# One queue for all the cache pages of a paged attention stage

## The reference, cut to what matters

```
past_ckv = cache_ckv[page_table].reshape(bd, -1, MLA_KV_RANK)     # 8 x 4096 x 256
past_kr = cache_krope[page_table].reshape(bd, -1, MLA_ROPE)       # 8 x 4096 x 64
s = einsum('bqhr,bkr->bhqk', qa, ckv) + einsum('bqhd,bkd->bhqk', qr, kr)   # scaled and masked
pr = softmax(s); o = einsum('bhqk,bkr->bqhr', pr, ckv)
```

## Time and profile before

| | |
|---|---|
| median of 3 runs | 1504.52 us (1503.92 to 1504.55) |
| the profiled execution | 1505.59 us, span 1503.9 us |
| TensorE matmul (PE), weight load (PEld) | 95%, 87% busy |
| DVE, ACT, POOL | 62%, 45%, 39% busy |
| mean granted TensorE clock | 0.986 |
| page loads | 128 by SP, 128 by POOL, 160 KB each |

### The profile page before, as it was taken

The page is one execution under the profiler, slowest core; times in us unless marked ns, Lnnn a source line. Parts: engine busy times, 40 slices in busy tenths (PEclk is TensorE's granted clock), DMA queues, the critical chain, the costliest instruction groups (busy, mean ns, idle before and its releaser), DMA issues.

```text
span 1503.9 us, 31274 instructions
## 1 busy us (share of the span) xinstructions
PE 1431.8 (95%) x11260; PEld 1311.3 (87%) x11260; DVE 926.1 (62%) x1496; ACT 672.3 (45%) x1263; POOL 585.2 (39%) x561
## 2 busy tenths in 40 slices
PE   6999999899999999998899999998979999999997
PEld 6999999789999999997886556666969999999996
DVE  4642447589999991326657744433469999994223
ACT  5333345355666672225412544443244666665211
POOL 2433113335555554431330044441315555554433
PEclk9999999999999999999999999999999999999998
DMA  4242322213232322223221089981213233223221
GB/s 162 71 141 85 118 80 99 85 48 112 99 112 84 112 77 97 77 92 109 79 95 39 1 261 285 284 260 47 72 47 112 85 112 100 96 76 99 94 96 66
DMA packets 55610, 160.20 MB, mean 107 GB/s; under 512 B 7553, under 2 KB 25474, under 8 KB 54226
## 3 DMA queue, kind: packets, MB, share of 16 engines
q1 hardware_dynamic: 49362, 137.82, 27.5%
q0 software_dynamic: 6144, 20.98, 4.6%
HBM read 150.72 MB, written 8.05 MB: 106 GB/s over the span
## 4 chain that ended last, share of the span: by engine, by line
PE 78%; DVE 12%; ACT 4%; issue 4%; POOL 1%; DMA 0%; SPq 0%; ACTq 0%; DVEq 0%; POOLq 0%
PE lin L2093 35%; PE lin L2381 23%; PE lin L2578 4%; PE px L2655 2%; PE px L2619 2%; PE px L2566 1%; PE px L2623 1%; DVE x L1538 1%; DVE tb L1532 1%; PE px L2586 1%; DVE xg_l L1354 1%; PE px L2158 1%; ACT w_h L793 1%; DVE xq_l L1676 1%; PE lin L2532 1%
## 5 line engine op out<-in xcount | busy, mean ns | idle before, releaser
L675 POOL TENSOR_TENSOR w_l<-w_raw,w_h 128x1024 fp32r<-128x1024 f32 (+1 forms) x62 | 177.2, 2859 | 339.0 <-ACT w_h L793 214.5
L2093 PE MATMUL lin<-xg_h,w_h 128*128 128x272 f32 x960 | 222.6, 307 | 32.9 <-DVE xg_l L1354 26.2
L2093 PE MATMUL lin<-xg_h,w_l 128*128 128x272 f32 x960 | 208.1, 292 | 0.0
L2093 PE MATMUL lin<-xg_l,w_h 128*128 128x272 f32 x960 | 208.1, 292 | 0.0
L2093 PEld LDWEIGHTS lin<-xg_h,w_h 128*128 128x128 f32 x960 | 157.4, 193 | 45.1 <-DVE xg_l L1354 19.9
L670 POOL TENSOR_TENSOR w_l<-w_raw,w_h 128x1024 fp32r<-128x1024 f32 (+2 forms) x39 | 98.0, 2514 | 220.1 <-ACT w_h L793 210.7
L793 ACT ACTIVATE w_h<-w_raw 128x1024 fp32r<-128x1024 f32 (+2 forms) x77 | 83.6, 1087 | 202.8 <-PE lin L2093 183.8
L2381 PE MATMUL lin<-xq_h,wq_r 128*128 128x272 f32 x864 | 170.1, 289 | 1.2 <-ACT part L1047 1.1
L2381 PE MATMUL lin<-xq_h,w_h 128*128 128x272 f32 x576 | 166.2, 288 | 0.2
L2381 PE MATMUL lin<-xq_h,w_l 128*128 128x272 f32 x576 | 166.0, 288 | 0.0
L2381 PE MATMUL lin<-xq_l,w_h 128*128 128x272 f32 x576 | 165.4, 287 | 0.0
(11 more groups left out here) (364 smaller groups left out, 3139.7 us busy)
## 6 DMA issues: line engine op xcount, KB each, us to landing
wq_raw<-w SPq DMA_DIRECT2D x36, 1024.0 KB, 4.9
w_raw<-w SPq DMA_DIRECT2D x67, 512.0 KB, 3.5
w_raw<-w SPq DMA_DIRECT2D x30, 704.0 KB, 4.1
pages<-cache SPq DMA_DIRECT2D x128, 160.0 KB, 3.8
pages<-cache POOLq DMA_DIRECT2D x128, 160.0 KB, 3.7
St<-state SPq DMA_DIRECT2D x4, 1024.0 KB, 5.8
gla_s<-St SPq DMA_DIRECT2D x4, 1024.0 KB, 3.9
w_raw<-w SPq DMA_DIRECT2D x4, 576.0 KB, 3.7
```

Of the source, the lines that this page charges most:

```text
L675: g.tensor_tensor(w_l[:, p % 2, 0:n], w_raw[:, p % 2, 0:n], w_h[:, p % 2, 0:n].bitcast(F32), ALU.subtract).then_inc(w_lo, 1)
L2093: last = mm(lin[:, 2 * out_set + half, 0:HALF], w[:, slot, (w0 + k) * P:(w0 + k + 1) * P], (v[ch] if isinstance(v, list) else v[:, ch, :]) ...
```

## The change

`load_pages` loses its two arguments and goes over all four pages of a group, with `pg_ready` for pages 0 and 2 and `pg_odd` for pages 1 and 3 as before. SP calls it in the same place. POOL's call goes; POOL goes on directly to the splits of the weight panels. The waits ahead of each group, the buffers, the bytes and TensorE's waits are the same.

```
-        def load_pages(eng, which, ready):
+        def load_pages(eng):
...
-                for j in which:
+                for j, ready in enumerate((pg_ready, pg_odd, pg_ready, pg_odd)):
                     page = eng.value_load(page_ids[0:1, 4 * g + j:4 * g + j + 1], min_val=0, max_val=io["n_pool"] - 1)
                     cols = slice(0, ROW) if j % 2 else slice(ROPE, ROPE + ROW)
                     eng.dma_start(pages[k][:, j * ROW:(j + 1) * ROW], io["cache"][page, :, cols]).then_inc(ready[k], 16)
...
-            load_pages(sp_, (0, 2), pg_ready)
+            load_pages(sp_)
...
-            load_pages(pool, (1, 3), pg_odd)
```

## The result

| | before | after |
|---|---|---|
| median | 1504.22 us (4 runs, 1503.81 to 1504.55) | 1628.39 us (4 runs, 1627.21 to 1629.66) |
| span of the profiled execution | 1503.9 us | 1627.1 us |
| mean granted clock | 0.986 | 0.961 |

The ratio is 1.0823, with a 95% interval of 1.081 to 1.0835: the changed kernel is slower by 124.2 us. The spans of the two profiled executions differ by 123.2 us.

A forecast was written before the change was run, and what follows sets the result against it. TensorE bounded the cached attention with loads hidden; with all pages on SP, its sequencer becomes the bound. Group 63's turn 123.3 us later plus 2.5 for the clock gives 125.8, forecast 1630 us, range 1619 to 1646.

The forecast's parts named there:

- Step 1: POOL loses 128 page issues in the cached attention and gains nothing, since it waits 24.0 us for ACT after its pages.
- Step 2: SP gains 128 issues; group 0's four pages need about 4.5 us, hidden in SP's 56.8 us wait for TensorE, costing nothing.
- Step 3: Groups 1 to 63 on SP: 251 intervals of 1.126 us from 866.37, last issue at 1149.0; the ring no longer holds SP.
- Step 4: The last page lands 2.4 us (2.3 to 3.8) after its issue, at 1151.4 us.
- Steps 5 and 7: TensorE's turn of group 63 starts 123.3 us later, work behind moving whole; SP's weight panels stay hidden behind POOL's split.
- Step 6: TensorE's clock falls in the sparse stage, free before the tail; in the tail it adds 2.5 us, bounds 0 and 5.8.
- what would show it: Signs in the profile after, among them TensorE busy about 2.54 of 4.50 us, 56%, through the cached-attention stage.
- The first rival: SP alone is quicker without POOL beside it, down to 0.830 us a page: 1553.5 us; chance 0.04.
- the second: DMA engines set the spacing, SP alone issues under 0.635 us a page, TensorE stays the bound: 1504.5 us; chance 0.02.
- the third: TensorE runs at the lower clock throughout and sets when group 63 is turned: 136.9 us later, 1641.4; chance 0.06.
- the fourth: The 6.8 us put down to TensorE are SP's own recurring pauses, interval 1.181 us: 1645.4 us; chance 0.08.

The follow-up runs named there:

- e2: Kernel before, but with three pages of a group loaded on SP and one on POOL: 1558.17 us, 52.1 more than before.
- e3: Changed kernel, but SP loads a page number only for pages 0 and 2, with all DMAs kept: 1556.35 us, 50.3 more than before.
- e5: Changed kernel without the assertion that the loaded page number lies in the pool: 1560.29 us, 68 less than the changed kernel.
- e6: Changed kernel, but one load fetches a group's four page numbers, and without the assertion: 1510.65 us, 1.0045 times before.
- e4: Changed kernel, but SP issues two DMAs a group, each with one number and 320 KB, the same bytes in all: 1504.91 us.
- e10: Changed kernel, but POOL beside SP goes through the same waits and loads all 256 numbers without issuing a DMA: 1630.46 us.
- e7: Changed kernel, but TensorE turns the latent blocks of groups 0 to 59 twice: 1630.37 us, 2 more than the changed kernel.

## Why the prediction was right

By its own steps, in the two profiled executions. No luck was needed: all terms but the last came out a little under the forecast, so nearly nothing cancels.

| step | predicted | measured |
|---|---|---|
| start of the long run (3) | 866.37 | 865.65 |
| 251 intervals (3) | 282.6 us, 1.126 each | 281.7 us, 1.1224 each |
| issue of the last page to TensorE's turn (4) | 2.4 us | 2.29 us |
| TensorE's turn of group 63 (5) | 1151.4, 123.3 later | 1149.67, 121.5 later |
| what the clock adds in the tail (6) | 2.5 us | 1.4 us |
| behind the stage (7) | 0 | 0.3 us |
| sum | 125.8 us | 123.2 us |

- Step 1: POOL's page work won nothing. It waits 366.7 us in one piece for ACT's split, which comes when it must.
- Step 2: SP's wait before group 1 shrank from 56.8 to 54.3 us, as the two more pages took of it.
- Step 3 carries the forecast and is shown from four sides: by count (e2), by instructions (e3, e5, e6), by bytes (e4) and by POOL's absence or presence (e10). It had split the time of before rightly into 6.8 us of ring waits and pauses of SP's own. The ring no longer binds (0.2 us).
- Step 4: the landing is 2.2 us where the DMA engines are 53% busy, against 3.8 at 90%; it is now on the path once, at the end.
- Steps 5 and 7 held: the work behind the turn of group 63 moved whole, and SP's weight panels still wait for POOL's split (17.4 us).
- Step 6 was right in kind and too large. The clock did fall through the stage, mean 0.84 to 0.85, and in the tail the values of unit 14 took 3.43 us in place of 1.86; but the scores behind them ran at full clock again (1.72 us for 16, as before), so that only one dense piece was hit: 16.1 us for the tail against 14.7. The tail by stretches (the clock is the third number from the end):

```profile
1151.00:1154.40 3.40, 3.40 (x34) 1.58 (x36) 0.46 (x1) 0.60 (x1) 0.00 (x0) 0.50 0.02 5
1154.40:1161.20 6.80, 4.06 (x57) 1.38 (x49) 1.83 (x6) 1.26 (x5) 0.00 (x0) 1.00 0.00 0
```

- One forecast in "what would show it" was off: TensorE's busy share is 70% (84.14 of 120.30), not 56%. The 56% took the matmuls at their full-clock length, and they are longer at the lower clock. It costs nothing, as SP is the bound.
- The first rival (SP quicker alone) falls with 1.1224 us and with e10; the second (not slower) with the result itself and with e4, which shows the DMA engines ready for nearly twice as much (261 GB/s against 147); the third (TensorE at the lower clock) with e2 and e7; the fourth (pauses of SP's own at 1.181) with the measured interval. The rule of the Trainium skill, "DMA: Bandwidth & Descriptors", "Issuing engines are not separate DMA queues", says that DMAs use the same 16 DMA engines whichever engine starts them, and that the sequencer's time to start one is usually small beside the DMA. The runs agree with the first: one queue took 89.7% of them (e4) where two took 45.1% and 44.5%. The second does not hold here: an issue with its number takes 1.10 us where the page lands in 2.2 us and TensorE uses it up in 0.635.

## What to carry to other kernels

What bounded this queue was its sequencer's time per DMA, and with an address from a table the fetching and checking of the number took more of it than the issue (0.58 of 1.10 us). Before moving DMAs to another queue, measure the interval between two issues on it without a wait (start to start, and over all of them, since the recorded durations add up to only three quarters of it), multiply by the DMAs per step, and compare with the step of the engine that now bounds: here 2 x 1.126 was under 2.54 and 4 x 1.126 was over. And if one queue must do it, widen what an issue brings (e4), load several numbers at once (e6), or see whether the check of each number can go (e5), before looking for a second queue.

## What I had not expected of the hardware

- Four page numbers load in 0.298 us where one takes 0.268.
- Leaving out an assertion with 0.17 us of recorded instructions shortens the interval by 0.28 us.
- POOL's queue, used alone, has an interval of 2.67 us in place of 1.157 every 72.0 us (three in the stage); SP's longest in the changed kernel is 1.87 us.
- The granted clock swings between its two levels in a stage where TensorE gets a group every 4.49 us (mean 0.84: 0.50 from 1055.4 to 1065.6 us, 1.00 from there to 1096.3), and hardly falls where it gets one every 3.37 (e2, 0.97 in the same window).
- Twice the bytes in a DMA lengthen SP's interval from 1.097 to only 1.135 us (e4).
